# Decay matrices of a state-space scan: running sums sent to all partitions through DRAM instead of being selected by matmuls

## The reference, cut to what matters

```python
def segsum_exp(a):
    cs = jnp.cumsum(a, axis=-1)
    diff = cs[..., :, None] - cs[..., None, :]
    mask = jnp.tril(jnp.ones((t, t), dtype=bool))
    return jnp.exp(jnp.where(mask, diff, -jnp.inf))

def ssd_chunked(xs, dt, a_neg, bm, cm):       # chunks of 128 tokens, 2 groups of 8 heads
    a_cs = jnp.cumsum(a, axis=-1)
    cb = jnp.einsum('bclgn,bcsgn->bcgls', cc, bc)
    m_mat = cb[:, :, :, None] * segsum_exp(a)           # the decay matrices
    y_diag = jnp.einsum('bcgels,bcsgep->bclgep', m_mat, xg)
    ...                                                  # states, y_off
    return y_diag + y_off
```

## Time and profile before

| | |
|---|---|
| median of three runs | 860.54 us (860.5 to 860.6) |
| the profiled execution's own time | 860.49 us |
| its span in the trace | 858.5 us |
| granted TensorE clock over the span | 0.997 |
| busy: PE, DVE, ACT, POOL | 99%, 72%, 62%, 22% |
| DMA | 146.21 MB, mean 170 GB/s |

### The profile page before, as it was taken

One profiled execution on the slowest core, in us unless ns is written; L12 is line 12 of the kernel. 1 busy time (PEld: TensorE's weight loads), 2 busy tenths in 40 slices (PEclk: granted clock), 3 DMA queues, 4 the chain that ended last, 5 costly groups with the idle time before them and its releaser, 6 DMA issues.

```text
span 858.5 us, 13054 instructions
## 1 busy us (share of the span) xinstructions
PE 850.3 (99%) x4645; PEld 706.5 (82%) x4645; DVE 619.9 (72%) x1125; ACT 534.5 (62%) x1031; POOL 185.5 (22%) x176
## 2 busy tenths in 40 slices
PE   9999999999999999999999999999999999999996
PEld 6877888778887888888888888887888888888885
DVE  6867866678776797677887546576797678877544
ACT  8667466765887864655565434787874655665432
POOL 0212053110152430023222000152330022222001
PEclk9999999999999999999999999999999999999998
DMA  9823563445534346655655655444347566555621
GB/s 328 281 57 136 174 205 120 148 147 176 163 132 147 122 135 211 207 178 181 194 195 176 219 196 174 151 146 147 101 146 220 186 186 194 185 179 182 230 108 50
DMA packets 94948, 146.21 MB, mean 170 GB/s; under 512 B 6564, under 2 KB 55204, under 8 KB 94884
## 3 DMA queue, kind: packets, MB, share of 16 engines
q1 hardware_dynamic: 92852, 139.58, 49.7%
q0 software_dynamic: 1296, 4.72, 1.6%
q10 hardware_dynamic: 736, 1.07, 0.3%
HBM read 144.32 MB, written 1.05 MB: 169 GB/s over the span
## 4 chain that ended last, share of the span: by engine, by line
PE 98%; DMA 0%; issue 0%; POOL 0%; DVE 0%; ACT 0%; SPq 0%; POOLq 0%; DVEq 0%
PE bank L1334 57%; PE bank L1292 17%; PE bank L1291 8%; PE bank L1217 6%; PE bank L1491 2%; PE bank L1419 1%; PE bank L1395 1%; PE bank L1392 1%; PE bank L1294 1%; PE bank L1422 1%; PE bank L1238 0%; DMA h<-in_x 0%; PE bank L1233 0%; PE bank L1481 0%; PE bank L1236 0%; PE bank L1498 0%
## 5 line engine op out<-in xcount | busy, mean ns | idle before, releaser
L1126 DVE TENSOR_TENSOR lo<-raw,hi 128x1024 fp32r<-128x1024 f32 x242 | 299.5, 1261 | 102.9 <-ACT hi L1510 102.6
L1510 ACT ACTIVATE hi<-raw 128x1024 fp32r<-128x1024 f32 (+1 forms) x258 | 266.7, 1058 | 125.7 <-PE bank L1334 68.2
L1334 PE MATMUL bank<-hi,xT 128*128 128x512 f32 (+2 forms) x800 | 251.9, 386 | 0.0
L1292 PE MATMUL bank<-xT,hi 128*128 128x512 f32 x640 | 220.5, 398 | 0.0
L1334 PEld LDWEIGHTS bank<-hi,xT 128*128 128x128 f32 x800 | 147.2, 188 | 30.8 <-issue 4.3
L1291 PE MATMUL bank<-xT,lo 128*128 128x256 f32 x560 | 157.4, 281 | 0.0
L1334 PE MATMUL bank<-lo,xT 128*128 128x512 f32 (+2 forms) x400 | 151.0, 378 | 0.0
L1292 PEld LDWEIGHTS bank<-xT,hi 128*128 128x128 f32 x640 | 114.9, 188 | 22.3
L1291 PEld LDWEIGHTS bank<-xT,lo 128*128 128x128 f32 x560 | 105.8, 189 | 3.4
L1334 PE MATMUL bank<-hi,hT 128*128 128x512 f32 x348 | 107.7, 389 | 0.0
L1334 PEld LDWEIGHTS bank<-lo,xT 128*128 128x128 f32 x400 | 75.4, 189 | 12.0
(11 more groups left out here) (286 smaller groups left out, 1153.5 us busy)
## 6 DMA issues: line engine op xcount, KB each, us to landing
raw<-in_w_in SPq DMA_DIRECT2D x26, 1024.0 KB, 5.1
raw<-in_w_gate SPq DMA_DIRECT2D x44, 512.0 KB, 4.0
raw<-in_w_up SPq DMA_DIRECT2D x44, 512.0 KB, 5.0
raw<-in_w_down SPq DMA_DIRECT2D x22, 1024.0 KB, 4.9
raw<-in_w_out SPq DMA_DIRECT2D x20, 1024.0 KB, 5.1
raw<-in_w_in_b SPq DMA_DIRECT2D x10, 1024.0 KB, 5.1
raw<-in_w_in_a SPq DMA_DIRECT2D x7, 1024.0 KB, 8.1
raw<-in_w_in_a SPq DMA_DIRECT2D x8, 256.0 KB, 5.6
```

The costliest lines, as they stand in the source:

```text
L1126: return engine.tensor_tensor(lo[r][:, cols], raw[c.i % RAW][:, cols], hi[r][:, cols].bitcast(F32), ALU.subtract)
L1292: last = nc.tensor.matmul(both, hi[r][:, still], xx[:, k, :, :], start=opens, stop=closes)
L1334: last = nc.tensor.matmul(bank[:, 0:wd], still[a], mv[r][:, off:off + wd], start=c.first and i == 0 and j == 0, stop=(c.last or c.closes a ...
L1510: nc.scalar.activation(hi[c.i % SPLIT][:, cols], raw[c.i % RAW][:, cols], ACT.Copy)\
```

## The change

The running sums are no longer selected by matmuls. TensorE forms them as 32 rows (16 heads of two token chunks) in one accumulation; VectorE negates them into `csum`, now fp32 and 32 x 128, in one operation. SyncE stores these rows to a DRAM tensor (`rows_out`) and sends four rows at a time to all 128 partitions of a buffer by a transfer with a repeated source (`spread`, eight for each layer, 256 KB each). GpSimd adds a mask of 0 or 1e30 in place (`cap`, eight for each layer, 128 x 512). ScalarE takes the exponential in place with scale -1. There are now eight buffers `MT`, one for each step of a layer, and the wait on the earlier diagonal product is gone, as are `picks` and its setup. Six transfers are issued before the projection z0, after SyncE has seen the last transposes of attention's probabilities (the buffers overlay them); the two of (1,0) follow later, after a wait on the last `conv`. In the output product `decays(1,0)` moves behind `z_silu`, and `weigh(1,0)` moves from O0's "after" slot to the end of O1's.

```diff
     def decays(g, m):
         for i in range(2):
-            bk = sc.bank()
-            s = sc.step("decay", q=i, mg=(m, g), bank=bk, sums=scan["sums"])
-            bk.freed = (s, "scalar")
-            scan["decay", g, m, i] = s
+            scan["decay", g, m, i] = sc.step("decay", q=i, mg=(m, g), of=scan["cap", g, m, i])
...
     b = halves(sc, w_in, [(x0 + 512, 512)], do(conv_silu, 0), att(2) + do(conv, 1, 0), do(conv, 1, 1))
+    sc.step("rows_out", layer=layer, sums=scan["sums"])
...
+    rows_spread(((0, 0), (0, 1), (1, 1)))
-    b = halves(sc, w_in, [(z0, 512)], do(conv_silu, 1), do(conv, 2, 0) + do(bback),
+    b = halves(sc, w_in, [(z0, 512)], do(conv_silu, 1), do(caps, 0, 0) + do(caps, 0, 1) + do(conv, 2, 0) + do(bback),
...
     b = halves(sc, w_in, [(z0 + 512, 512)], do(decays, 0, 0) + do(weigh, 0, 0),
-               do(decays, 0, 1) + do(weigh, 0, 1), do(scanned, 0, 0) + do(back, 1) + do(low_at_once))
+               do(caps, 1, 1) + do(decays, 0, 1) + do(weigh, 0, 1),
+               do(rows_spread, ((1, 0),)) + do(scanned, 0, 0) + do(back, 1) + do(low_at_once))
...
-        0: (do(squared, 0, 1) + do(group_mean, 0) + do(decays, 1, 0) + do(weigh, 1, 1) + do(group_norm, 0),
-            do(z_silu) + do(weigh, 1, 0)),
-        1: (do(turn_y, 0, 0) + do(scanned, 1, 1), do(turn_y, 0, 1) + do(squared, 1, 1)),
+        0: (do(squared, 0, 1) + do(group_mean, 0) + do(caps, 1, 0) + do(weigh, 1, 1) + do(group_norm, 0),
+            do(z_silu) + do(decays, 1, 0)),
+        1: (do(turn_y, 0, 0) + do(scanned, 1, 1), do(turn_y, 0, 1) + do(squared, 1, 1) + do(weigh, 1, 0)),
...
+                if s.kind == "rows_out":
+                    ended(sp, s.sums, "vector")
+                    sp.dma_start(decay_rows[s.layer], csum[:, :]).then_inc(rows_stored, 16)
+                if s.kind == "spread":
+                    n, (m, g) = s.i % 8, s.mg
+                    if n == 0:
+                        sp.wait_ge(rows_stored, 16 * (s.layer + 1))
+                        for x in s.att["flip"][-3:]:
+                            ended(sp, x, "tensor")
+                    if n == 6:
+                        ended(sp, s.before, "tensor")
+                    row = SH * m + 8 * g + 4 * s.q
+                    sp.dma_start(Hb[f"MT{n}"][:, :, :], decay_rows[s.layer, row:row + 4].partition_broadcast(P))\
+                      .then_inc(spread_in[n], 16)
...
-                for i in range(4):
-                    hh = 8 * g + 4 * (s.q % 2) + i
-                    last = nc.tensor.matmul(bank[:, i * P:(i + 1) * P], picks[0:KSEL, hh, :], csum[0:KSEL, m, :],
-                                            start=True, stop=True)
...
-                act.wait_ge(sem["decay", "tensor"], s.i + 1)
-                if s.i >= 4:
-                    act.wait_ge(sem["diag", "tensor"], s.i - 3)
+                ended(act, s.of, "gpsimd")
                 for i in range(4):
                     hh = 8 * g + 4 * (s.q % 2) + i
-                    last = nc.scalar.activation(Hb[f"MT{s.i % 4}"][:, i, :], psum[4 + s.bank.at][:, i * P:(i + 1) * P],
-                                                ACT.Exp, bias=Hb["ncs"][:, m, hh:hh + 1])
+                    mt = Hb[f"MT{s.i % 8}"][:, i, :]
+                    last = nc.scalar.activation(mt, mt, ACT.Exp, scale=-1.0, bias=Hb["ncs"][:, m, hh:hh + 1])
...
+            if s.kind == "cap":
+                pool.wait_ge(spread_in[s.i % 8], 16 * (s.of.layer + 1))
+                ended(pool, s.sums, "vector")
+                nc.gpsimd.tensor_tensor(mt, mt, spread(Hb["later"][:, :].unsqueeze(1), [P, 4, P]), ALU.add)\
+                  .then_inc(sem["cap", "gpsimd"], 1)
...
-                chained(copy(csum[0:96, :, :], left[0:96]))
-                chained(tt(left[0:96], left[0:96], csum[0:96, :, :], ALU.subtract))
-                copy(csum[32:64, :, :], left[32:64])
-                chained(copy(csum[64:96, :, :], left[64:96]))
-                chained(tt(left[64:96], left[64:96], csum[64:96, :, :], ALU.subtract))
-                done(copy(csum[64:96, :, :], left[64:96]), s)
+                if s.i == 0:
+                    ts(Hb["later"][:, :], upper, NEG, -NEG, ALU.mult, ALU.add)
+                done(ts(csum[:, :], bank[0:2 * SH, 64:64 + P], -1.0, None, ALU.mult), s)
```

More of the change, by code:

```diff
@@ L50 @@
 SINE_AT, TABLES_AT, ALOG_AT = 13, 21, 18
-PICKS_AT = 24
 POOL_SPLITS = 6
@@ L70 @@
 C_MASK = C_KEEP
[L71 to L75, removed]
+C_ALL = C_MASK + 2 * QC
 def constants():
@@ L104, in constants @@
             c[:, at:at + P] = np.where(x, 0.0, NEG)
[L105 to L109, removed]
     return c
@@ L586, in conv @@
         bk = sc.bank()
-        s = sc.step("conv", j=j, u=u, bank=bk, ev=scan["ev", j], layer=layer,
+        s = scan["conv", j, u] = sc.step("conv", j=j, u=u, bank=bk, ev=scan["ev", j], layer=layer,
                     conv=scan["silu", j - 1] if j else None)
@@ L613, in sums, with rows_spread, caps @@
         bk.freed = (scan["sums"], "vector")
+    def rows_spread(groups):
+        for g, m in groups:
+            for i in range(2):
+                scan["spread", g, m, i] = sc.step("spread", q=i, mg=(m, g), layer=layer, att=a, before=scan.get(("conv", 2, 1)))
+    def caps(g, m):
+        for i in range(2):
+            scan["cap", g, m, i] = sc.step("cap", q=i, mg=(m, g), of=scan["spread", g, m, i], sums=scan["sums"])
     def decays(g, m):
         for i in range(2):
-            bk = sc.bank()
-            s = sc.step("decay", q=i, mg=(m, g), bank=bk, sums=scan["sums"])
-            bk.freed = (s, "scalar")
-            scan["decay", g, m, i] = s
+            scan["decay", g, m, i] = sc.step("decay", q=i, mg=(m, g), of=scan["cap", g, m, i])
     def weigh(g, m):
@@ L895 @@
     "bback": ("tensor", "scalar", "vector"), "xback": ("tensor", "scalar", "gpsimd"),
-    "decay": ("tensor", "scalar"), "weigh": ("vector",), "diag": ("tensor",), "off": ("tensor",),
+    "decay": ("scalar",), "cap": ("gpsimd",), "spread": (), "rows_out": (), "weigh": ("vector",), "diag": ("tensor",), "off": ("tensor",),
     "join": ("vector",), "ysquare": ("scalar",), "ynorm": ("vector",), "final": ("vector",), "scaled": ("vector",), "part_sum": ("vector",), "tail_square": ("vector",), "tail_added": ("vector",), "pool_scaled": ("gpsimd",),
@@ L1039, in plan @@
             put("MT3", [P, 4, P], where=e)
-            put("da", [P, M, 3, M * SH], where=b["z_at"])
+            b["MT4"], b["MT5"] = decays[:, 0], decays[:, 1]
+            e = put("MT6", [P, 4, P], where=b["xin_at"])
+            put("MT7", [P, 4, P], where=e)
+            put("da", [P, M, M * SH], where=b["z_at"])
             put("xs", [P, M, SSM])
@@ L1047, in plan @@
                 e = put(name, [P, M, SH], where=e)
+            put("later", [P, P], BF16, where=e)
             e = small_at
@@ L1084, in build @@
     warm_up = nc.alloc_semaphore("warm_up")
-    picks_made = nc.alloc_semaphore("picks_made")
+    rows_stored = nc.alloc_semaphore("rows_stored")
+    spread_in = [nc.alloc_semaphore(f"spread_in{i}") for i in range(8)]
     gain_in = nc.alloc_semaphore("gain_in")
@@ L1472, in _ @@
                 last.then_inc(sem["xback", "tensor"], 1)
[L1473 to L1478, removed]
-                for i in range(4):
-                    hh = 8 * g + 4 * (s.q % 2) + i
-                    last = nc.tensor.matmul(bank[:, i * P:(i + 1) * P], picks[0:KSEL, hh, :], csum[0:KSEL, m, :],
-                                            start=True, stop=True)
-                last.then_inc(sem["decay", "tensor"], 1)
             elif s.kind == "diag":
@@ L1490, in _ @@
                     c0 = (4 * (s.q % 2) + i) * HD
-                    last = nc.tensor.matmul(bank[:, c0:c0 + HD], Hb[f"MT{s.decay.of.i % 4}"][:, i, :],
+                    last = nc.tensor.matmul(bank[:, c0:c0 + HD], Hb[f"MT{s.decay.of.i % 8}"][:, i, :],
                                             Hb["xg"][:, s.m, hh * HD:(hh + 1) * HD], start=True, stop=True)
@@ L1982, in _ @@
                     tables()
-                if s.kind == "chunk" and s.i == PICKS_AT:
-                    pick_tables()
                 if s.low_waits:
@@ L2229, in _ @@
                 for m in range(M):
-                    nc.vector.memset(Hb["da"][:, m, :, SH * (1 - m):SH * (2 - m)], 0.0)
-                    last = tt(Hb["da"][:, m, :, SH * m:SH * (m + 1)], spread(Hb["dt"][:, m, :].unsqueeze(1), [P, 3, SH]),
-                              spread(small[:, s.layer, 1, :].unsqueeze(1), [P, 3, SH]), ALU.mult)
+                    nc.vector.memset(Hb["da"][:, m, SH * (1 - m):SH * (2 - m)], 0.0)
+                    last = tt(Hb["da"][:, m, SH * m:SH * (m + 1)], Hb["dt"][:, m, :], small[:, s.layer, 1, :], ALU.mult)
                 done(last, s)
```

24 lines of the change are left out of this document (10 added, 14 removed).

## The result

The changed kernel takes **869.9 us** (median of 4 runs, 869.7 to 870.9) beside 860.6 for the kernel before: 1.011 times as long, 95% interval 1.010 to 1.012. I had said 863.5, with 866.0 as the upper end. The direction was right, the size was three times mine: +9.3 us in place of +3.0.

What follows compares the result with a forecast made beforehand. TensorE, busy 99% of the span, was taken as the bound. Its 2.1 us saving a layer, cut to 0.7 by y, became 1.5 us lost through weigh(1,0): two layers +3.0, 860.49 to 863.5 us, range 858.8 to 866.0.

Steps and rivals of the forecast that it cites:

- TensorE's saving: TensorE's queue: dropping 64 decay matmuls saves 2.1 us a layer, 4.2 us in the program.
- First thing late, y: Output product, first transposes of y: TensorE arrives before y is written; 0.7 us a layer of its saving left.
- Second thing late, weigh(1,0): VectorE ahead of the (1,0) product: weigh behind a full queue starts the product 1.5 us later than before.
- the sign that I had set down for it: Trace after: TensorE idle about 2 us before the first (1,0) product, ended by VectorE's weigh; its absence refutes (C).
- (C): The forecast itself: weigh(1,0) late behind VectorE's full queue, 863.5 us, bounds 862.5 to 864.7; chance 0.64.
- The table's price: ScalarE between silu and exponentials of (1,0): one more table load per layer, taken as 1.4 us.
- Transfers: Spreads to GpSimd's caps: four early caps end between 275 and 283, ahead of xback at 283.08, so covered.
- (A): Rival: nothing waits and TensorE's whole saving comes through, 856.3 us; chance 0.08.
- (B): Rival: the (1,0) product finds its factor in time and only y holds TensorE, 859.1 us; chance 0.13.
- (D): Rival: a transfer lands late for GpSimd, delaying xback, for example 866.0 us; chance 0.15 together with (E).
- (E): Rival: GpSimd's caps hold VectorE at places costed at nothing, 2 us more; chance 0.15 together with (D).

Runs made afterwards that it cites:

- e9: e8 with TensorE's first transposes of y placed behind the products of (1,1), decays still not computed: 858.3 us.
- e7: Changed kernel without GpSimd's caps; ScalarE waits for the transfers itself, exponentials with another scale and bias, so decays are wrong: 868.4 us.
- e1: Changed kernel with the two caps of (1,0) on GpSimd ahead of xback(1), not behind the power: 870.6 us.
- e2: Changed kernel with the exponentials of (1,0) and weigh(1,0) back at their old places: 868.7 us.
- e10: e3 with TensorE's first transposes of y placed behind the products of (1,1), nothing left out: 860.8 us.
- e14: Changed kernel with the caps of (1,0) in GpSimd's gap ahead of the power: 869.1 us.
- e3: Changed kernel with the edits of both e1 and e2: 863.5 us.
- e8: e7 with the exponentials and weigh of (1,0) at their old places, decays still not computed: 860.4 us.
- e4: Kernel before the change with two idle 128 x 512 GpSimd operations behind the power of group 0: 862.4 us.
- e13: e11 with the caps of (1,0) moved into GpSimd's gap ahead of the power: 861.1 us.
- e11: e2 with TensorE's first transposes of y placed behind the products of (1,1), nothing left out: 864.2 us.

## Why the prediction was wrong in size

**TensorE's saving: right.** 2.1 us a layer were to bring TensorE to y at 309.3; e9 has it there at 309.42, the changed kernel at about 309.8 (its last product ahead of the stop starts at 309.59).

**First thing late, y: the mechanism was right, the term mis-sized.** I had the two caps of (1,0) behind the power in the text, and costed them only on the write of y, which they hardly touch. What they hold are the two small operations between power and write, +1.87 us. I had the join 0.2 to 0.26 us earlier and it is 0.83 later, 0.5 of it by the change: ScalarE's exponentials from SBUF take 2.35 us a set where they took 1.99, so 0.35 and not my 0.1, and VectorE's weigh waits 0.48 us for them at 296.32. y was to come at 310.2 to 311.0 and a stop of 0.7 us (0.4 to 1.2) was to be left; the stop is 2.95.

**The step that failed: nothing followed from a stop but its own length.** The prediction treats TensorE's idle time as time lost once. Behind a stop of 2.95 us the engine ran 6.83 us at half clock, 3.4 us a layer, 6.8 of the 9.3. It is not in the sum, not in the rivals, and the range ended 3.9 us short for it. No row of before shows the price, since TensorE never stops there for more than some tenths between its first product and its last. But the trace of before does show the fall: TensorE's last matmul starts at 851.39, and from 854 to the end the granted clock is 0.50. A forecast with two stops in it should have had a rival with the clock in it.

**Second thing late, weigh(1,0): right elsewhere, absent here.** The extra table load is there (311.16 in the changed kernel, 1.28 us), the split behind the exponentials starts at 315.88 (I had about 315), and the wait of 2.2 us before the product appears in e7 as 2.09 and in e1 as 2.10. In the changed kernel it is gone, because TensorE is so late itself, and undoing it gives nothing back that the runs can show (e2). By the sign that I had set down for it, a wait before the product, (C) is wrong for this kernel. That y delays TensorE by 1.5 us a layer, as much as I had for the weigh, is luck.

**The table's price.** ScalarE in the changed kernel:

```profile
310.08 1.06 ACT L1629 ACTIVATE hyb_z<-hyb_z 128x1024 f32<-128x1024 f32 x1
311.16 1.28 ACT L1785 ACT_TABLE_LOAD   x1
312.45 2.45 ACT L1785 ACTIVATE hyb_MT<-hyb_MT,hyb_ncs 128x128 f32<-128x128 f32 x8
```

From the silu to the exponentials are 2.37 us. Before, the operation behind the silu started 0.97 us after it, so the switch costs 1.40, the 1.4 that I took. The Trainium skill ("ScalarE: Activation LUTs", "What ACT_TABLE_LOAD costs") has 2.66; the load agrees, and the drain shows no more here than in the kernel before.

**Transfers: right.** The four early caps start at 271.09, straight behind a split on GpSimd, and last 6.52 us; xback starts at 283.35 (0.27 later than in the earlier trace rows, no more than the difference at 261) and waits for ScalarE and not for them. The transfers of 256 KB land in 4.9 us (median of 12, 5.3 of the other four).

**The shape of the rivals.** (A) and (B) couldn't hold with y that late. (D) didn't happen. (E), GpSimd's caps on VectorE's path, did: I bounded it by half a cap each, four on the path, 2 us; the four are there, two in each layer between the power and y, but at nearly a whole cap each, 3.7 us.

## What to carry to other kernels

Where a change takes work from TensorE, find the next producer in line and work out its lateness to the end of the queue. A stop of TensorE of nearly 3 us was paid again behind it in half clock every time here, shorter ones sometimes, so cover a stop with products that are ready (e9) and take it as a term of its own in the sum. Work handed to GpSimd is not free for VectorE even where both are idle on the average: by these runs, price each 128 x 512 operation at about 0.9 us of VectorE's chain wherever VectorE reads two operands from SBUF beside it. Here TensorE's saving was real, but even without the caps only 2.7 of its 4.2 us came through (e9), and with them the best complete order (e10) only comes out even with the kernel before.

## What the runs showed of the hardware

**The clock behind a stop.** Stops of 2.94 to 2.98 us: 6.83 us at 1.2 GHz in both layers of the changed kernel and of e14 and in one of e2, 3.41 in the other. Stops of 1.4 to 2.1 us (e1, e3, e7, e8): 3.41 us or none, once 6.83 where two stops followed each other, and not the same from run to run. A stop of 0.6 us (e4), and those of 0.3 to 0.8 in e9, e10 and e13: none. Longer stops cost more, but these runs settle no limit: e11, with a stop of 2.43 us in each layer, has the full clock behind both in its profile, at 864.2 us, while two of its other runs took 866.4 with a mean clock of 0.995.

**VectorE beside GpSimd.** An operation of GpSimd that takes 1.04 us alone costs VectorE's chain 0.7 to 1.0 us beside it, and 0.16 becomes 1.11. In the same stretches VectorE's operations that read PSUM keep their 0.68 us (303.69 in the changed kernel, with xback beside it). The Trainium skill says this in "SBUF — State Buffer", "Who interferes with whom": a VectorE instruction with two inputs in SBUF contends with a GpSimd instruction that reads SBUF, and the pair of ports that they share is an exclusive lock. The trace agrees: 0.16 becomes 1.11 beside a cap of about 1.1. In e4 a TENSOR_SCALAR (L2088, 0.90), which has one tensor input, is held as well; the same section of the Trainium skill lists that operation among those that can contend in a faster mode of VectorE, and whether L2088 ran in it no run here shows.

**ScalarE from SBUF.** Eight exponentials of 128 x 128 take 2.35 us from start to start of what follows with SBUF as source, 1.99 from PSUM.
